# Head norms by narrow matmul tiles, key copies ahead of weight casts, and attention one fill later, in a two-block model step

## The chip, the cores and the metric

The kernel runs on one core of a Trainium2 chip. The metric is the device time of one execution in microseconds. Engines are called as in the profile: PE (TensorE, the matmuls; PEld is its weight load), DVE (VectorE), ACT (ScalarE), POOL (GpSimd), SP (SyncE, which here issues the transfers). Each engine runs its own instruction list in the written order, and the lists are tied together by semaphores alone.

## What is computed

A sequence of 256 tokens of width 1024 goes through two blocks. The change touches the second block only, where a wide projection feeds three branches that are then gated and added:

```
def hgrn2_branch(zq, zi, zf_fwd, zf_bwd, zg, lb, gnorm, w_o):
    ...
    o = one_direction(zf_fwd, lb[0], False) + one_direction(zf_bwd, lb[1], True)
    o = rmsnorm_2(o.transpose(0, 2, 1, 3), gnorm)     # per head: o * rsqrt(mean(o*o) + 1e-6) * gnorm
    gate = jax.nn.silu(zg.astype(f32)).reshape(o.shape)
    o = (o * gate).reshape(b, t, HG_WIDTH).astype(dt)
    return o @ w_o

merged = sigmoid(g_hg) * y_hg + sigmoid(g_na) * y_na + sigmoid(g_ca) * y_ca
```

There are 8 heads of 128 channels in the first branch (HGRN2, "hg"), whose one_direction is a gated scan over the tokens with a decay of its own for each channel, 8 heads of 64 in a neighbourhood attention ("na") and 4 heads of 128 in an attention over 256 memory vectors ("ca").

## The kernel before

**Weights.** All weights come in one order from device memory, as blocks of 128 x 128, 8 to a unit. SP loads two units at a time into `raw` (line 539). ACT rounds a unit into `w_hi` (line 667), then DVE (line 1075) or POOL (line 630) makes the rest, `w_lo`. PE takes the blocks in order and multiplies three times for each: high by high, high by low, low by high (lines 1625 and 1656). `w_hi` and `w_lo` hold four units, so ACT can round a unit only when PE is through with the one four places before; `feed(target)` in ACT's, DVE's and POOL's lists does all units up to a target. Which engine makes `w_lo` is set by a table: DVE for everything in the stretch up to fill ("cq", 1), POOL for the fills mhg 0 and 1 and for all mca and mna fills, both in turn for the rest.

**Fills.** A fill is one bank of PSUM written by PE (16 blocks, 48 three-pass products, or 12 blocks and 36 in the mca and mna fills) and read by ACT or DVE. `wait_fill` in ACT's list first feeds the units whose places the first half of the fill frees, waits for the fill, and feeds the unit that its second half frees. The fills concerned come in the order hi 0-3, hg 0-3, nq 0-1, nk 0-1, nv 0-1, cq 0-1 (the side fills, numbered e = 0 to 15), then mhg 0-7, mca 0-7, mna 0-7 (the merge fills, i = 0 to 23).

**Levels.** The scan of the first branch is done in 7 levels of doubling width, each after a side fill (`LEVEL_AFTER`: levels 0 to 6 after e = 1, 3, 5, 7, 9, 11, 12). For levels 0 to 4 ACT copies keys from `k_fb` into `gate_tmp` and `k_mix` (`level_keys`, line 723) once DVE's `grow` of the level before is done, and PE multiplies from them (line 1883). In ACT's `wait_fill` these copies stand behind the cast of the fill's first half.

**Head norms.** After e = 13, PE's `hg_values` makes the outputs of two heads at a time (g = 0 to 3, lines 1905 and 1906) in PSUM bank `sc[g]`; ACT squares them (929) and copies them out (930); PE multiplies the squares by a 128 x 128 matrix of 1/128 (1912), which puts the mean into all 128 partitions; ACT takes the root (933), DVE the reciprocal (1434), and DVE multiplies the gated outputs by it (1438, gating in 1428). ACT rounds the product into `o_hg_s` (`hg_hi_part`, 938) and DVE makes its low half (1089). The merge fill mhg 0 needs all of `o_hg_s` in its second half.

**Attention.** The 12 heads (4 ca, then 8 na) go through a pipeline in slots: in slot i PE makes the scores of head i (1950; for na two heads at a time, 1939), transposes head i-1's probabilities (1960) and multiplies head i-2's by the values (1985, 1975). DVE finds the maxima (1463, 1465) and normalizes (1470, 1472), ACT takes the exponentials (969). Slot 0 stands before mhg 0 and slot i+1 after merge fill i.

## Time and profile before

| | us |
|---|---|
| median of 3 runs | 934.26 |
| lowest and highest | 931.34, 935.6 |
| the profiled execution's own time | 935.25 |
| its span, first to last instruction | 933.4 |
| PE busy in it | 903.3 |
| DVE, ACT, POOL busy in it | 671.3, 507.1, 305.0 |

The trace's clock starts at the first instruction, so that its end, 933.4, lies 1.85 us under the profiled execution's own time. A matmul's end is modelled, and successive matmuls overlap: the pitch from one start to the next is the price, not the duration. In float32 one product of the program is two MATMUL rows in the trace.

### The profile page before, as it was taken

What the parts mean: (1) busy time and instruction counts of PE and PEld (TensorE: products, weight loads), DVE (VectorE), ACT (ScalarE), POOL (GpSimd) and SP (SyncE); (2) the same over time, 40 slices, a digit from 0 to 9 for tenths busy, and PEclk for the clock granted to TensorE, in tenths of its full rate; (3) what the DMA queues carried; (4) which work ended last, traced back from release to release, by engine and by line L of the source; (5) the groups of instructions that cost most, each with busy time, mean ns of one, the idle gap of its engine ahead of it and who ended that gap; (6) DMA issues with size and microseconds to landing.
All of it is one profiled execution on the core that took longest, in us unless ns stands there. A gap on an engine that the chain in (4) does not pass through costs nothing.

```text
span 933.4 us, 16400 instructions
## 1 busy us (share of the span) xinstructions
PE 903.3 (97%) x6848; PEld 816.5 (87%) x6848; DVE 671.3 (72%) x836; ACT 507.1 (54%) x748; POOL 305.0 (33%) x115
## 2 busy tenths in 40 slices
PE   7998999999999999999999999999999999999996
PEld 7988986888888878999999998998999888888885
DVE  4999677888883257668778778876555589999622
ACT  6544637544554356655554675555545466666542
POOL 2000000565565410000000004845785156666542
PEclk9999999999999999999999999999999999999998
DMA  9583453655555545545535444344455365555551
GB/s 358 208 259 119 147 207 123 236 181 183 191 201 193 190 171 180 180 153 177 197 110 182 161 96 175 137 136 136 136 204 181 137 207 190 192 194 186 185 176 45
DMA packets 31801, 163.78 MB, mean 175 GB/s; under 512 B 9169, under 2 KB 10977, under 8 KB 13296
## 3 DMA queue, kind: packets, MB, share of 16 engines
q1 hardware_dynamic: 31664, 162.66, 50.8%
q8 instruction: 54, 0.88, 0.4%
q14 instruction: 19, 0.16, 0.0%
q0 software_dynamic: 64, 0.08, 0.0%
HBM read 161.32 MB, written 1.42 MB: 174 GB/s over the span
## 4 chain that ended last, share of the span: by engine, by line
PE 80%; DVE 12%; ACT 3%; DMA 2%; issue 1%; SPq 1%; DVEq 0%; ACTq 0%
PE ring L1625 27%; PE acc L1703 18%; PE acc L1637 9%; PE ring L1637 9%; PE acc L1638 4%; PE ring L1638 4%; DVE w_lo L1075 3%; PE ring L1656 3%; DVE conv_y L1167 3%; DMA raw<-wstream 2%; PE acc L1883 1%; ACT w_hi L667 1%; DVE y L1127 1%; DVE ret_inv L1241 1%; ACT sq L673 1%
## 5 line engine op out<-in xcount | busy, mean ns | idle before, releaser
L630 POOL TENSOR_TENSOR w_lo<-raw,w_hi 128x1024 fp32r<-128x1024 f32 x100 | 287.7, 2880 | 595.3 <-ACT w_hi L667 595.1
L667 ACT CAST w_hi<-raw 128x1024 fp32r<-128x1024 f32 x284 | 297.2, 1051 | 312.5 <-PE ring L1625 127.8
L1075 DVE TENSOR_TENSOR w_lo<-raw,w_hi 128x1024 fp32r<-128x1024 f32 x184 | 227.7, 1251 | 112.6 <-ACT w_hi L667 102.3
L1625 PE MATMUL ring<-h,w_hi 128*128 128x256 f32 x1408 | 259.2, 286 | 3.5 <-DVE w_lo L1075 1.8
L1625 PEld LDWEIGHTS ring<-h,w_hi 128*128 128x128 f32 x1408 | 220.8, 192 | 7.3 <-issue 6.4
L1625 PE MATMUL ring<-h,w_lo 128*128 128x256 f32 x704 | 199.9, 284 | 1.1 <-issue 1.1
L1625 PEld LDWEIGHTS ring<-h,w_lo 128*128 128x128 f32 x704 | 135.5, 192 | 0.0
L1637 PE MATMUL acc<-h,w_hi 128*128 128x512 f32 x352 | 124.7, 397 | 0.8 <-DVE h L1133 0.8
L1637 PE MATMUL ring<-h,w_hi 128*128 128x512 f32 x352 | 124.2, 396 | 0.0
L1638 PE MATMUL acc<-h,w_lo 128*128 128x256 f32 x352 | 98.2, 279 | 0.0
L1638 PE MATMUL ring<-h,w_lo 128*128 128x256 f32 x352 | 98.2, 279 | 0.0
L1703 PE MATMUL acc<-w_hi,ff 128*128 128x512 f32 x352 | 94.3, 390 | 0.0
L1637 PEld LDWEIGHTS acc<-h,w_hi 128*128 128x128 f32 x352 | 66.1, 188 | 17.1 <-DVE h L1133 1.0
L1637 PEld LDWEIGHTS ring<-h,w_hi 128*128 128x128 f32 x352 | 66.1, 188 | 15.9
L1703 PEld LDWEIGHTS acc<-w_hi,ff 128*128 128x128 f32 x352 | 65.8, 188 | 13.8 <-DVE w_lo L1075 0.3
L1289 DVE TENSOR_TENSOR ff<-prod_tmp,ff 128x256 fp32r<-128x256 f32 x44 | 67.2, 1530 | 0.9 <-ACT ff L1038 0.9
L1638 PEld LDWEIGHTS acc<-h,w_lo 128*128 128x128 f32 x352 | 66.2, 188 | 0.2 <-issue 0.2
L1638 PEld LDWEIGHTS ring<-h,w_lo 128*128 128x128 f32 x352 | 66.2, 188 | 0.0
L1703 PE MATMUL acc<-w_lo,ff 128*128 128x512 f32 x176 | 54.2, 389 | 0.0
L1656 PE MATMUL ring<-w_hi,h 128*128 128x256 f32 x256 | 48.3, 291 | 0.8 <-ACT v_ret L740 0.8
L1656 PEld LDWEIGHTS ring<-w_hi,h 128*128 128x128 f32 x256 | 41.0, 197 | 1.7 <-ACT v_ret L740 1.0
L1703 PEld LDWEIGHTS acc<-w_lo,ff 128*128 128x128 f32 x176 | 33.0, 188 | 7.0
(252 smaller groups left out, 1269.9 us busy)
## 6 DMA issues: line engine op xcount, KB each, us to landing
raw<-wstream SPq DMA_DIRECT2D x142, 1024.0 KB, 4.9
toep_t<-toep SPq DMA_DIRECT2D x16, 96.0 KB, 3.2
u<-uconv SPq DMA_DIRECT2D x4, 284.0 KB, 6.5
x<-x_tok SPq DMA_DIRECT2D x2, 512.0 KB, 5.1
mem<-mem_tok SPq DMA_DIRECT2D x1, 1024.0 KB, 11.8
w_ple<-wproj SPq DMA_DIRECT2D x1, 1024.0 KB, 6.9
out_t<-y SPq DMA_DIRECT2D x4, 256.0 KB, 2.2
decay<-decay_tab SPq DMA_DIRECT2D x1, 768.0 KB, 6.4
```

The source lines that it names most:

```text
L630: nc.gpsimd.tensor_tensor(w_lo[:, u % UNITS], unit_of_raw(u), as_f32(w_hi[:, u % UNITS]), ALU.subtract).then_inc(lo_ready["pool"], 1)
L667: nc.scalar.copy(w_hi[:, u % UNITS], unit_of_raw(u)).then_inc(hi_ready, 1)
L673: A(spare_out, src, ACT.Square, scale=1.0 / 32.0, accum_out=sums[:, 0, n:n + 1]).then_inc(mean_ready, 1)
L1075: V.tensor_tensor(w_lo[:, u % UNITS], unit_of_raw(u), as_f32(w_hi[:, u % UNITS]), ALU.subtract).then_inc(lo_ready["dve"], 1)
L1127: V.scalar_tensor_tensor(out=y_tok[:, tt, c], in0=src[:, tt, c], scalar=r, in1=gain[name][:, c], op0=ALU.mult, op1=ALU.mult).then_inc(sign ...
L1167: ins = V.scalar_tensor_tensor(out=conv_y[:, j], in0=src, scalar=weight, in1=conv_y[:, j], op0=ALU.mult, op1=ALU.add)
L1289: V.tensor_tensor(ff[:, 1, j], prod_tmp[:, j % 2], as_f32(ff[:, 0, j]), ALU.subtract).then_inc(ff_ready, 1)
L1625: last = mm(dst, w[a], src[:, b, kt], start=n == 0 and i == 0, stop=n == kts - 1 and i == 2)
L1637: mm(both, w[0], h_both[:, kt].rearrange("p a s -> p (a s)"), start=kt == 0, stop=False)
L1638: last = mm(b[:, i, 0], w[1], h[:, 0, kt], start=False, stop=kt == KT - 1)
L1656: last = mm(b[:, tt], src[:, xa, kt, tt * P:tt * P + P], ws[kt][wa], start=kt == 0 and i == 0, stop=kt == KT - 1 and i == 2)
L1703: last = mm(acc[:, tt, 512 * g:512 * g + 512], src(b, i, tt), w[:, u % UNITS, 4 * g:4 * g + 4].rearrange("p a b -> p (a b)"), start=i == 0 ...
```

## The change

It makes five edits.

1. In ACT's `wait_fill` the key copies of a level come before the cast of the fill's first half.
2. The head means of four heads go into one group of matmuls that use only 32 columns of the matrix each and write to 32 partitions each of bank `st` (`hg_mean`), once for heads 0 to 3 behind the third pair of outputs and once for heads 4 to 7 behind the fourth.
3. ACT's root and DVE's reciprocal work on that compact form: two of 128 x 256 each instead of four of 128 x 512. `hg_spread_roots`, behind fill cq 0, multiplies each head's 32 rows of it by 32 rows of 1/128, so that a quarter of the root lands in all 128 partitions of `sc`; DVE multiplies by it and by 4 (`spread_root` names the place).
4. The rounding of `o_hg_s` in ACT and its low half in DVE move behind fill cq 0, all four pairs in a row.
5. Attention slot i stands after merge fill i. `att_scores` of the first two heads waits for all of `hg_out`.

```diff
--- before.py
+++ after.py
@@ -494,6 +495,11 @@
         NHEADS = len(HEADS)
         MERGE_FILLS = [(name, j) for name, j, _, _ in FILLS if name in ("mhg", "mna", "mca")]
 
+        def spread_root(g):
+
+            banks = acc[:, g % 2].rearrange("p (b c) -> p b c", b=2)
+            return banks[:, :, g // 2 * S:g // 2 * S + S]
+
         def unit_of_raw(u):
             return raw[:, (u // 2) % RAW, UB * (u % 2):UB * (u % 2) + UB]
 
@@ -725,10 +731,10 @@
             def wait_fill(name, j, behind=True):
 
                 n = fi(name, j)
-                feed(split_target(n))
                 side = n - fi("hi", 0)
                 if LEVEL_AFTER.get(side, MASKED) < MASKED:
                     level_keys(LEVEL_AFTER[side])
+                feed(split_target(n))
                 act.wait_ge(pe_step, fill_step(n))
                 if behind:
                     feed(behind_target(n))
@@ -922,16 +928,15 @@
                                    sc[g][:].rearrange("p (a b) -> p a b", a=2)).then_inc(st_cross, 1)
 
             def hg_outputs():
-                for g in range(5):
-                    if g < 4:
-                        act.wait_ge(sc_done, SC_HGO + g + 1)
-                        o = sc[g][:].rearrange("p (a b) -> p a b", a=2)
-                        A(hg_sq[:, 2 * g:2 * g + 2], o, ACT.Square).then_inc(hg_squares, 1)
-                        nc.scalar.copy(o_hg[:, 2 * g:2 * g + 2], o).then_inc(o_copied, 1)
-                    if g:
-                        act.wait_ge(hg_stat, g)
-                        A(hg_sq[:, 2 * g - 2:2 * g], sc[g - 1][:].rearrange("p (a b) -> p a b", a=2), ACT.Sqrt,
-                          bias=eps[:, 0:1]).then_inc(hg_root, 1)
+                for g in range(4):
+                    act.wait_ge(sc_done, SC_HGO + g + 1)
+                    o = sc[g][:].rearrange("p (a b) -> p a b", a=2)
+                    A(hg_sq[:, 2 * g:2 * g + 2], o, ACT.Square).then_inc(hg_squares, 1)
+                    nc.scalar.copy(o_hg[:, 2 * g:2 * g + 2], o).then_inc(o_copied, 1)
+                    if g >= 2:
+                        half = slice((g - 2) * S, (g - 1) * S)
+                        act.wait_ge(hg_stat, g - 1)
+                        A(rstd[:, half], st[:, half], ACT.Sqrt, bias=eps[:, 0:1]).then_inc(hg_root, 1)
 
             def hg_hi_part(g):
                 act.wait_ge(hg_out, g + 1)
@@ -954,9 +959,9 @@
                 if e == CROSS_AFTER:
                     cross()
                     hg_outputs()
-                if e >= CROSS_AFTER:
-                    hg_hi_part(e - CROSS_AFTER)
-            hg_hi_part(3)
+                if e == CROSS_AFTER + 1:
+                    for g in range(4):
+                        hg_hi_part(g)
 
             def att_exp(a):
 
@@ -999,7 +1004,6 @@
                 act.wait_ge(merge_full, j + 1)
                 nc.scalar.copy(merged_s[:, 0, j], merged[:, j]).then_inc(merge_hi, 1)
 
-            att_slot(0)
             for i, (name, j) in enumerate(MERGE_FILLS):
                 wait_fill(name, j)
                 wait_gate_slot(act, name, j)
@@ -1007,7 +1011,7 @@
                 A(gate_tmp[:, gate_slot(name, j), 0], bank(name, j)[:, 0], ACT.Tanh, scale=0.5).then_inc(gate_done, 1)
                 if i >= 17:
                     merge_split(i - 17)
-                att_slot(i + 1)
+                att_slot(i)
             merge_split(7)
             prime(ACT.Sqrt)
             feed(end_unit("wout2"))
@@ -1421,24 +1425,27 @@
                     grow(LEVEL_AFTER[e])
                 if e == CROSS_AFTER:
                     gated = []
-                    for g in range(6):
+                    for g in range(4):
+                        dve.wait_ge(o_copied, RET + g + 1)
+                        o = o_hg[:, 2 * g:2 * g + 2]
+                        gated.append(link(V.scalar_tensor_tensor(out=o, in0=o, scalar=col("gnorm"),
+                                                                 in1=gate_hg[:, 2 * g:2 * g + 2],
+                                                                 op0=ALU.mult, op1=ALU.mult)))
+                        if g >= 2:
+                            half = rstd[:, (g - 2) * S:(g - 1) * S]
+                            dve.wait_ge(hg_root, g - 1)
+                            V.reciprocal(half, half).then_inc(hg_inv, 1)
+                if e == CROSS_AFTER + 1:
+                    for g in range(5):
                         if g < 4:
-                            dve.wait_ge(o_copied, RET + g + 1)
+                            dve.wait_ge(hg_spread, 1)
+                            after(gated[g])
                             o = o_hg[:, 2 * g:2 * g + 2]
-                            gated.append(link(V.scalar_tensor_tensor(out=o, in0=o, scalar=col("gnorm"),
-                                                                     in1=gate_hg[:, 2 * g:2 * g + 2],
-                                                                     op0=ALU.mult, op1=ALU.mult)))
-                        if 1 <= g < 5:
-                            dve.wait_ge(hg_root, g)
-                            root_g = hg_sq[:, 2 * g - 2:2 * g]
-                            V.reciprocal(root_g, root_g).then_inc(hg_inv, 1)
-                            dve.wait_ge(hg_inv, g)
-                            after(gated[g - 1])
-                            o = o_hg[:, 2 * g - 2:2 * g]
-                            V.tensor_tensor(o, o, root_g, ALU.mult).then_inc(hg_out, 1)
-                        if g >= 2:
-                            dve.wait_ge(hg_hi, g - 1)
-                            lo_part(o_hg_s, o_hg[:, 2 * g - 4:2 * g - 2], 2 * g - 4, 2 * g - 2).then_inc(hg_split, 1)
+                            V.scalar_tensor_tensor(out=o, in0=spread_root(g), scalar=4.0, in1=o, op0=ALU.mult,
+                                                   op1=ALU.mult).then_inc(hg_out, 1)
+                        if g:
+                            dve.wait_ge(hg_hi, g)
+                            lo_part(o_hg_s, o_hg[:, 2 * g - 2:2 * g], 2 * g - 2, 2 * g).then_inc(hg_split, 1)
 
 
             def att_logits(a):
@@ -1483,9 +1490,6 @@
                 dve.wait_ge(o_att, n + 1)
                 V.tensor_tensor(o[:, 1, t], sc[3][:, 0:S], as_f32(o[:, 0, t]), ALU.subtract).then_inc(att_ready, 1)
 
-            att_logits(0)
-            att_norm(0)
-
             def merge_lo(j):
                 dve.wait_ge(merge_hi, j + 1)
                 V.tensor_tensor(merged_s[:, 1, j], merged[:, j], as_f32(merged_s[:, 0, j]), ALU.subtract
@@ -1494,8 +1498,8 @@
             added = {}
             for i, (name, j) in enumerate(MERGE_FILLS):
                 gates[0] += 1
-                if i + 1 < NHEADS:
-                    att_logits(i + 1)
+                if i < NHEADS:
+                    att_logits(i)
                 feed_behind(name, j)
                 wait_gate(gates[0])
                 yv = bank(name, j)[:, 1]
@@ -1519,10 +1523,10 @@
                         ins.then_inc(merge_full, 1)
                     else:
                         added[i] = link(ins)
-                if i + 1 < NHEADS:
-                    att_norm(i + 1)
-                if 2 <= i + 1 < NHEADS + 2:
-                    att_lo(i - 1)
+                if i < NHEADS:
+                    att_norm(i)
+                if 2 <= i < NHEADS + 2:
+                    att_lo(i - 2)
                 if i >= 17:
                     merge_lo(i - 17)
             merge_lo(7)
@@ -1895,24 +1899,44 @@
                                   start=True, stop=True)
                     last.then_inc(sc_done, 1)
 
+            def hg_value(g):
+
+                pe.wait_ge(st_cross, g + 1)
+                for a in range(2):
+                    hd = 2 * g + a
+                    o = sc[g][:, a * S:a * S + S]
+                    mm(o, v_hg[:, 0, hd * P:hd * P + P], st_hg[:, hd, 0:S], start=True, stop=False)
+                    last = mm(o, v_hg[:, 1, hd * P:hd * P + P], st_hg[:, hd, S:2 * S], start=False, stop=True)
+                last.then_inc(sc_done, 1)
+
+            def hg_mean(half):
+
+                pe.wait_ge(hg_squares, 2 * half + 2)
+                if half:
+                    pe.wait_ge(hg_root, 1)
+                for n in range(4):
+                    last = mm(st[32 * n:32 * n + 32, half * S:half * S + S], mat("m128")[:, 0:32],
+                              hg_sq[:, 4 * half + n], start=True, stop=True)
+                last.then_inc(hg_stat, 1)
+
             def hg_values():
-                for g in range(5):
-                    if g < 4:
-                        pe.wait_ge(st_cross, g + 1)
-                        for a in range(2):
-                            hd = 2 * g + a
-                            o = sc[g][:, a * S:a * S + S]
-                            mm(o, v_hg[:, 0, hd * P:hd * P + P], st_hg[:, hd, 0:S], start=True, stop=False)
-                            last = mm(o, v_hg[:, 1, hd * P:hd * P + P], st_hg[:, hd, S:2 * S], start=False, stop=True)
-                        last.then_inc(sc_done, 1)
-                    if g:
-                        pe.wait_ge(hg_squares, g)
-                        pe.wait_ge(o_copied, RET + g)
-                        for a in range(2):
-                            last = mm(sc[g - 1][:, a * S:a * S + S], mat("m128"), hg_sq[:, 2 * (g - 1) + a],
-                                      start=True, stop=True)
-                        last.then_inc(hg_stat, 1)
-
+
+                for g in range(3):
+                    hg_value(g)
+                hg_mean(0)
+                hg_value(3)
+                hg_mean(1)
+
+            def hg_spread_roots():
+
+                pe.wait_ge(o_copied, RET + 4)
+                for half in range(2):
+                    pe.wait_ge(hg_inv, half + 1)
+                    for n in range(4):
+                        rows = slice(32 * n, 32 * n + 32)
+                        last = mm(sc[n][:, half * S:half * S + S],
+                                  mat("m128")[rows], rstd[rows, half * S:half * S + S], start=True, stop=True)
+                last.then_inc(hg_spread, 1)
 
             for e, (name, j) in enumerate(SIDE_FILLS):
                 if name in ("hi", "nv"):
@@ -1927,6 +1951,8 @@
                     cross()
                     wait_read(pe, "hi", 3)
                     hg_values()
+                if e == CROSS_AFTER + 1:
+                    hg_spread_roots()
 
             def att_scores(a):
                 kind, i = HEADS[a]
@@ -1942,7 +1968,7 @@
                                 last.then_inc(scored, 1)
                     return
                 if a < 2:
-                    pe.wait_ge(hg_root, 4)
+                    pe.wait_ge(hg_out, 4)
                     wait_read(pe, "cq", 1)
                 else:
                     pe.wait_ge(exp_ready, a - 1)
@@ -1994,7 +2020,6 @@
                 if 2 <= i < NHEADS + 2:
                     att_values(i - 2)
 
-            att_slot(0)
             for i, (name, j) in enumerate(MERGE_FILLS):
                 b = open_fill(name, j)
                 tile_out(b[:, 0], h)
@@ -2006,7 +2031,7 @@
                 else:
                     pe.wait_ge(att_ready, 8)
                     tile_out(b[:, 1], o_na, 4)
-                att_slot(i + 1)
+                att_slot(i)
 
             def merged_kt(i, tt):
                 if tt == 0:
```

ACT's list around the side fill e = 3 and the level behind it; `v_hg` is the fill's copy, `gate_tmp` and `k_mix` the key copies, `w_hi` the weight casts. Before:

```order
L740 COPY v_hg<-ring 128x2x256
L667 CAST w_hi<-raw 128x1024
L723 COPY gate_tmp<-k_fb 128x1024
L723 COPY k_mix<-k_fb 128x1024
L667 CAST w_hi<-raw 128x1024
```

After:

```order
L746 COPY v_hg<-ring 128x2x256
L729 COPY gate_tmp<-k_fb 128x1024
L729 COPY k_mix<-k_fb 128x1024
L673 CAST w_hi<-raw 128x1024 x2
L746 COPY v_hg<-ring 128x2x256
```

The two key copies stand ahead of the cast that they stood behind.

PE's list where the head outputs (`acc<-st_hg,v_hg`) and means (`hg_sq,con`) are made, from the third pair of heads on. Before:

```order
L1912 MATMUL acc<-hg_sq,con 128x256 x2
L1905 MATMUL acc<-st_hg,v_hg 128x256
L1906 MATMUL acc<-st_hg,v_hg 128x256
L1905 MATMUL acc<-st_hg,v_hg 128x256
L1906 MATMUL acc<-st_hg,v_hg 128x256
L1912 MATMUL acc<-hg_sq,con 128x256 x4
L1625 MATMUL ring<-h,w_hi 128x256 x2
```

After, with the spread of the roots behind fill cq 0:

```order
L1918 MATMUL ring<-hg_sq,con 32x256 x4
L1908 MATMUL acc<-st_hg,v_hg 128x256
L1909 MATMUL acc<-st_hg,v_hg 128x256
L1908 MATMUL acc<-st_hg,v_hg 128x256
L1909 MATMUL acc<-st_hg,v_hg 128x256
L1918 MATMUL ring<-hg_sq,con 32x256 x4
...
L1629 MATMUL ring<-h,w_lo 128x256
L1937 MATMUL acc<-rstd,con 128x256 x8
L1629 MATMUL ring<-h,w_hi 128x256 x2
```

Eight products over 128 columns became eight over 32, in two groups, and eight products from 32 rows were added between fills cq 0 and cq 1.

ACT's list from the last root to the first merge fill; `q_ca` is the copy of a cq fill, `o_hg_s` the rounding of a pair of heads. Before:

```order
L933 ACTIVATE hg_sq<-acc,eps 128x512 x2
L938 CAST o_hg_s<-o_hg 128x512
L667 CAST w_hi<-raw 128x1024 x2
L740 COPY q_ca<-ring 128x512
L938 CAST o_hg_s<-o_hg 128x512
L667 CAST w_hi<-raw 128x1024 x2
L740 COPY q_ca<-ring 128x512
L938 CAST o_hg_s<-o_hg 128x512 x2
L969 ACT_TABLE_LOAD
```

After:

```order
L939 ACTIVATE rstd<-ring,eps 128x256
L673 CAST w_hi<-raw 128x1024 x2
L746 COPY q_ca<-ring 128x512
L943 CAST o_hg_s<-o_hg 128x512 x4
L673 CAST w_hi<-raw 128x1024 x2
L746 COPY q_ca<-ring 128x512
L673 CAST w_hi<-raw 128x1024 x2
L1011 ACT_TABLE_LOAD
```

All four roundings stand between the copies of cq 0 and cq 1, ahead of the two weight casts of the fill mhg 1, and attention's exponential is no longer ahead of the first merge fill's casts.

## Rows read from the trace of the kernel before

**Rows 1.** The page's part 1: busy us (share), instructions.

```profile
PE 903.3 (97%) x6848; PEld 816.5 (87%) x6848; DVE 671.3 (72%) x836; ACT 507.1 (54%) x748; POOL 305.0 (33%) x115
```

**Rows 2.** PE's waits, 440 to 720 us: who waited for whom, us, times, longest.

```profile
PE acc L1883 <- issue: 1.8, 1, 1.8
PE acc L1950 <- ACT q_ca L740: 1.8, 1, 1.8
PE ring L1625 <- issue: 1.1, 1, 1.1
PE acc L1883 <- ACT gate_tmp L723: 1.0, 1, 1.0
PE acc L1960 <- DVE probs L1472: 0.5, 1, 0.5
PE acc L1912 <- ACT o_hg L930: 0.4, 1, 0.4
...
PE acc L1883 <- ACT k_mix L723: 0.2, 1, 0.2
```

**Rows 3.** Stretches behind e = 1: us; busy PE, PEld, DVE, ACT, POOL; clock, DMA, GB/s.

```profile
460.90:462.70 1.80, 0.02 (x2) 0.00 (x0) 0.34 (x1) 1.80 (x3) 0.00 (x0) 1.00 0.00 0
...
464.20:467.40 3.20, 3.20 (x17) 3.20 (x17) 3.20 (x4) 0.00 (x0) 0.00 (x0) 0.50 0.83 294
```

**Rows 4.** Timeline at e = 3, ACT (start, us, engine, line, operation, [idle before]).

```profile
475.56 1.05 ACT L667 CAST w_hi<-raw 128x1024 fp32r<-128x1024 f32 x1 [2.79 <-PE ring L1656]
476.52 1.23 ACT L723 COPY gate_tmp<-k_fb 128x1024 f32<-128x1024 f32 x1
477.64 1.18 ACT L723 COPY k_mix<-k_fb 128x1024 f32<-128x1024 f32 x1
```

**Rows 5.** Chain of work through the head norms: start, us, what.

```profile
550.61 0.67 PE acc L1905 x2
...
559.51 0.60 ACT hg_sq L929
560.11 0.49 ACT o_hg L930
...
560.73 1.10 PE acc L1912 x4
561.83 11.52 PE ring L1625 x96
```

**Rows 6.** An earlier group of 32-column products: ns min/median/max, first and last start.

```profile
L1737 PE MATMUL acc<-u,w_conv x128: 377/379/405, 64.9 to 71.6; 128*32 128x256 f32 x128
```

**Rows 7.** The chain at attention's scores: ca and na.

```profile
581.96 0.87 PE acc L1950 x4
...
604.84 1.06 PE acc L1939 x8
```

**Rows 8.** Timeline at the end of fill cq 1, ACT and PE.

```profile
573.43 1.04 ACT L667 CAST w_hi<-raw 128x1024 fp32r<-128x1024 f32 x1 [1.83 <-PE ring L1625]
574.38 0.58 ACT L740 COPY q_ca<-ring 128x512 f32<-128x512 f32 x1
...
575.10 1.10 PE L1950 MATMUL acc<-mem_k,q_ca 128*128 128x256 f32 x4 [1.77 <-ACT q_ca L740]
```

**Rows 9.** DVE and POOL in the head norms.

```profile
556.11 3.35 DVE L1434 RECIPROCAL hg_sq<-hg_sq 128x512 f32<-128x512 f32 x1
569.40 2.37 DVE L1438 TENSOR_TENSOR o_hg<-o_hg,hg_sq 128x512 f32<-128x512 f32 x1
...
568.79 2.42 POOL L630 TENSOR_TENSOR w_lo<-raw,w_hi 128x1024 fp32r<-128x1024 f32 x1 [0.43 <-ACT w_hi L667]
```

**Rows 10.** DVE and POOL at head 10, behind merge fill i = 9.

```profile
647.96 0.76 DVE L1455 SCALAR_TENSOR_TENSOR probs<-acc,toep_t 128x256 f32<-128x256 f32 x2 [2.01 <-PE acc L1939]
649.47 1.81 DVE L1465 TENSOR_SCALAR soft<-soft 128x2 f32<-128x2 f32 x1
652.64 0.62 DVE L1472 TENSOR_SCALAR probs<-probs,soft 128x256 f32<-128x256 f32 x2
...
646.51 4.74 POOL L630 TENSOR_TENSOR w_lo<-raw,w_hi 128x1024 fp32r<-128x1024 f32 x2 [2.92 <-ACT w_hi L667]
```

1 line of the change is left out of this document (added).

## The prediction

> **What bounds the kernel now.** The page's first part comes first: PE is busy 903.3 of 933.4 us, the next engine 671.3 [rows 1]. So PE's own list is the bound, the time is its work plus its gaps, and an edit is worth what it takes out of one or the other; time saved on DVE or ACT counts only where PE waits for it. The second view is PE's waits over the stretch that the change touches, 440 to 720 us [rows 2]. They are eight, 7.1 us together, of which the rows show seven: 1.8 and 1.1 us for "issue" (nothing that the profile shows), 1.8 for the copy of `q_ca`, 1.0 and 0.2 for key copies, 0.5 for normalized probabilities, 0.4 for the last copy of a head output. Third, the stretches around the largest gap [rows 3]: PE does nothing from 460.9 to 462.7, and from 464.2 to 467.4 the granted clock is 0.50, that is 1.2 GHz instead of 2.4. Fourth, the chain and the timelines at the places that the diff moves [rows 4, 5, 8, 10].
>
> **Key copies first.** At e = 3 ACT casts a unit at 475.56 for 1.05 us, having idled 2.79 us for PE to free its place, and only then copies keys, until 478.82 [rows 4]. PE waits 1.0 and 0.2 us for them [rows 2]. In the new order the copies can run in ACT's 2.79 idle microseconds: they take 1.23 + 1.18 = 2.4, so they end before the cast can start, and the cast is not later than now. Both waits go: **-1.2 us**. At e = 5, 7 and 9 PE shows no wait for keys, so there is nothing to win; there the casts stand up to 2 us later, and what hides that is the four-unit lead (the unit belongs to the fill after next, over 5 us away). If this cover failed, PE would wait out the rest, at most 2 us at each of three places. At e = 1 the 1.8 us gap falls inside the level's products too, but its row names no copy, so I leave it and the low clock behind it as they are (rival one).
>
> **Means in narrow tiles.** Before, the mean of one head is two MATMUL rows of 128 x 256 at full price. The price is the pitch, which the chain shows as 0.87 us for 4 rows, 0.217 each [rows 7]. Eight heads are 16 rows, 3.45 us. In the new form each product uses 32 columns. The trace has such a group, the packed convolution: 128 rows of 32 columns by 256 start between 64.9 and 71.6, 6.7 / 127 = 0.053 us each, four times as dense [rows 6]. Two groups of 8 rows are then 2 x 0.43; I add 0.15 to 0.2 to each for going into and out of it: the na scores, 8 rows in 1.06 us [rows 7], are 0.19 over 8 x 0.108. That makes 2 x 0.6 = 1.2 us, 2.2 less than now. The wait for ACT changes too. Before, PE waits for the square (0.60) and the copy (0.49) of the last pair, partly filled by another pair's mean, 0.4 us net [rows 2, 5]. Now it needs only the square, but nothing stands in between: 0.60 and some 0.15 to get there and back, 0.75 us. ACT's first compact root is done by then, since it follows the third pair's copy. Sum: -2.2 + 0.35, **-1.9 us**. Bounds: if the groups ran at the full 0.217, they would take 3.45 again and the edit would cost 0.35; at the best, without the 0.2s, it gives 2.3.
>
> **The spread.** New work on PE, between cq 0 and cq 1: eight products from 32 rows, 16 MATMUL rows. No row of the trace has 32-row tiles with 128 columns. Nearest are the na scores, 64 rows and 128 columns, two tiles at once: 8 in 1.06 us, 0.133 each [rows 7]; and the 32-column group at 0.053 [rows 6]. Four different row groups and four banks are used here, so I take 16 x 0.053 + 0.2 = **+1.1 us**. At the two-tile pitch it is 2.1, at the full pitch 16 x 0.217 = 3.5, and nothing excludes that; the low end is 0.85. It waits for DVE's reciprocals, and these have time: a reciprocal of 128 x 512 takes 3.35 us [rows 9], two of half the size the same together, and fill cq 0 gives some 5.8 us (the two cq fills take 11.52, [rows 5]). The 10 us that DVE saves (13.4 of reciprocals become 3.4) are on no path of PE.
>
> The Trainium skill, page "TensorEngine Tiling (Array Packing)", Key Properties, speaks against edits 2 and 3: changing the tiling mode drains the engine. There are six changes here. The measured na group bounds what two of them cost, 0.19 us, and that is in the sum; a price per drain is on no such row, and at a whole matmul's duration of 0.38 each, as in [rows 6], the six would be 2.3 us instead of 0.6.
>
> **Casts behind, and q_ca.** Before, attention's slot 0 follows fill cq 1 at once. PE waits 1.77 us, because ACT casts a unit first (until 574.47) and copies `q_ca` then [rows 8]. In the new order fill mhg 0 starts there, and needs only weights that were cast long before: **-1.8 us**. What is late next? mhg 0's second half, 2.9 us in, needs `o_hg_s`. By the sums above cq 0 ends at about 565.4, the spread at 566.5. DVE then has four products and four low halves of 0.6 to 0.75 us, 5.4 us, and one hold-up: the row at 569.40 took 2.37 us and ended when POOL's cast of 568.79 to 571.21 was through [rows 9], where such a row alone takes 0.69. So the last low half is ready by about 574, and the first pair by 570. PE enters mhg 0 at some 572.3 and its second half at 575.2, taking the pairs one after another: covered by 1 us for the last and 5 for the first. In ACT the four roundings hold the queue until about 572; behind them stand the two casts of mhg 1, with POOL's low parts (2.4 us each) behind these: done by 578.1, needed from 579 and 582. If the cover is gone, PE waits for POOL, one low part of 2.4 us at most. SP's loads wait for these low parts in turn; they are for units four fills on.
>
> The Trainium skill, "SBUF — State Buffer", Who interferes with whom, says that a DVE operation with both inputs in SBUF and a GpSimd operation lock each other out for a whole instruction. The trace agrees (2.37 against 0.69). By this rule the new product, with one input in PSUM, is free of it and only the low halves can be held up.
>
> **Attention a fill later.** No work is added. The wait of 0.5 us at head 10 [rows 2] has this build: its scores come behind fill i = 9, the next fill is a short one, and DVE's scaling of the maxima (1.81 us for 128 x 2 values) sat behind POOL's double cast 646.51 to 651.25 [rows 10]. In the new order the even na heads 8 and 10 follow fills 8 and 10, where POOL has one cast and then a pause, so this hold-up passes to the odd heads, which have one slot more. Worked through, heads 8, 9 and 11 come out with about 0.4 us to spare. I take **-0.2 us**, between -0.5 and +1.
>
> **Sum.** -1.2 - 1.9 + 1.1 - 1.8 - 0.2 = -4.0 us on the profiled span of 933.4, or 935.25 with what lies around it. The median of the runs is 934.26, 1 us under the profiled execution. The saving is the same: 930.3.
>
> **Rivals.**
> 1. *The gap at e = 1 goes too.* For it: the copies for level 0 stand at that place, and the order there changes. PE would win the 1.8 us gap and what the 1.2 GHz cost (half of 3.4 us, 1.7). 930.3 - 3.5 = 926.8. Against it: PE's list is the same up to there, the gap lies in mid-group, and the row says "issue".
> 2. *The narrow tiles do not overlap.* The spread costs 2.1 to 3.5 instead of 1.1: 931.3 to 932.7, "no change". For it: no row shows this shape.
> 3. *The q_ca wait comes back at mhg 0,* as a wait for `o_hg_s` or for mhg 1's weights: the 1.8 us are given back, 932.1. This is the case in which the edit doesn't do what it says. For it: four pairs in a row on one path PE-DVE-ACT-DVE with 1 us of cover. Against: DVE has little else there.
> 4. *Attention becomes late, and the change is slower.* One more na pair works beside the short fills, where POOL is busy more than half of the time. If each of heads 8 to 11 meets a POOL cast in its scaling and another in its normalization, that is 2 x 2.4 less the 0.4 of cover, 4.4 us a head, 17.6 in all, 947.9 at worst. Slower by over 0.5% (938.9) begins at 8.6 us of new waits, so it decides when half of these hold-ups happen: 939 and more. Against it: before, three of the four heads had no wait at all.
>
> **How the numbers follow.** Chances: the forecast 0.50, rival one 0.15, two 0.15, three 0.15, four 0.05. A measurement of this kernel can tell about 0.5% from no change, 4.7 us here; the line is at 929.6. The forecast lies 0.7 above the line, and with 1.5 us of doubt in its terms and in two medians it falls below it in somewhat under half of its cases (0.5 x 0.45 = 0.23). With rival one that is 0.38 for faster. Rivals two and three and the rest of the forecast are 0.57, rival four 0.05 for slower. The range goes from rival one (926.6) to the dear end of rival two (933.0). The forecast's own range is 928.8 to 931.8.
>
> **What would show it.** In the changed profile: no PE wait for `gate_tmp` or `k_mix` behind e = 3; two groups of 8 MATMUL rows on `hg_sq` with starts 0.05 us apart, one wait of 0.75 us for the last square; the 16 rows on `rstd` within 1.1 us; no wait for `q_ca`, nor for `o_hg_s`, between fill cq 1 and the end of mhg 1; the 1.8 us "issue" gap and the 0.50 clock still behind e = 1; PE's waits for normalized probabilities under 0.5 us in all. The forecast is wrong if the gap at e = 1 is gone, if the rows on `rstd` start over 0.1 us apart, or if PE's waits grow between 640 and 665 us.

## The result and the profile after

| | before | after |
|---|---|---|
| median of 6 runs, us | 934.6 | 928.38 |
| lowest and highest | 931.34, 935.6 | 926.34, 929.86 |
| the profiled execution's own time | 935.25 | 929.86 |
| its span | 933.4 | 928.0 |

The ratio is 0.9934, with a 95% interval from 0.9916 to 0.9952, so 4.5 to 7.9 us less. The second set of six runs of the same changed kernel (`after_again`, below) gives 0.9947 [0.9929, 0.9964]. The change is faster by about 0.6%; the forecast was 4.0 us, 0.43%.

The page of the kernel after, part 1, answers to [rows 1]; PE has 16 MATMUL rows more, the spread:

```profile
PE 901.5 (97%) x6864; PEld 813.9 (88%) x6864; DVE 663.8 (72%) x834; ACT 506.1 (55%) x746; POOL 304.7 (33%) x115
```

PE's waits of the kernel after, 440 to 720 us (who waited for whom, us, times, longest), answer to [rows 2]. L1887 is a level, L1629 the fill, L1918 a mean, L1908 a head output:

```profile
PE acc L1887 <- issue: 1.9, 1, 1.9
PE ring L1629 <- issue: 0.8, 1, 0.8
PE ring L1918 <- ACT hg_sq L934: 0.7, 1, 0.7
PE acc L1908 <- ACT st_hg L927: 0.3, 1, 0.3
```

Four waits are left of eight. Both key waits, the one for `q_ca` and the one for the probabilities are gone, the one for a head's copy has become one for its square, as foreseen. No wait stands for `o_hg_s`, mhg 1's weights or the roots. What remains is mostly "issue".

ACT at e = 3, timeline of the kernel after, answers to [rows 4]:

```profile
474.81 0.58 ACT L746 COPY v_hg<-ring 128x512 f32<-128x512 f32 x1
475.29 1.26 ACT L729 COPY gate_tmp<-k_fb 128x1024 f32<-128x1024 f32 x1
476.43 1.18 ACT L729 COPY k_mix<-k_fb 128x1024 f32<-128x1024 f32 x1
478.18 1.05 ACT L673 CAST w_hi<-raw 128x1024 fp32r<-128x1024 f32 x1 [0.57 <-PE ring L1660]
```

The copies take 2.3 us of the time in which ACT had idled 2.79; 0.57 us of idle time is left ahead of the cast, which is still released by PE. So the cast isn't later for them.

The head norms in the chain of work of the kernel after (start, us, what), answering to [rows 5], and the spread's rows (ns min/median/max, first to last start):

```profile
551.49 0.67 PE acc L1908 x2
...
556.91 0.57 PE ring L1918 x8
...
559.44 0.61 ACT hg_sq L934
560.04 0.04 issue
560.09 0.64 PE ring L1918 x8
560.73 5.94 PE ring L1629 x48
566.67 1.08 PE acc L1937 x16
```

```profile
L1937 PE MATMUL acc<-rstd,con x16: 374/374/478, 566.6 to 567.4; 32*128 32x256 f32 x16
```

From the first head output to fill cq 0 it is 560.73 - 551.49 = 9.24 us in the chain now, and cq 0 began at 561.83 - 550.61 = 11.22 in [rows 5]. Of these 1.98 us, 0.28 are the modelled end of the last mean, which the chain counts: from the start of the first output's row to the start of the first row of cq 0 it is 10.87 before and 9.17 now, 1.70 less. In the chain the two groups of eight take 0.57 and 0.64 us, and the sixteen rows of the spread 1.08. By the starts of the same rows of cq 0 and cq 1 (11.57 us before, 12.75 now) the spread costs 1.18.

DVE and ACT behind fill cq 0 and POOL beside them, timelines of the kernel after; [rows 8, 9] are the places before:

```profile
567.81 1.29 DVE L1444 SCALAR_TENSOR_TENSOR o_hg<-acc,o_hg 128x512 f32<-128x512 f32 x2 [4.75 <-PE acc L1937]
569.19 1.65 DVE L1093 TENSOR_TENSOR o_hg_s<-o_hg,o_hg_s 128x512 fp32r<-128x512 f32 x1
570.76 0.68 DVE L1444 SCALAR_TENSOR_TENSOR o_hg<-acc,o_hg 128x512 f32<-128x512 f32 x1
...
572.56 1.46 DVE L1093 TENSOR_TENSOR o_hg_s<-o_hg,o_hg_s 128x512 fp32r<-128x512 f32 x2
```

```profile
573.20 2.00 ACT L673 CAST w_hi<-raw 128x1024 fp32r<-128x1024 f32 x2
```

```profile
567.88 2.41 POOL L636 TENSOR_TENSOR w_lo<-raw,w_hi 128x1024 fp32r<-128x1024 f32 x1 [0.48 <-ACT w_hi L673]
574.33 4.78 POOL L636 TENSOR_TENSOR w_lo<-raw,w_hi 128x1024 fp32r<-128x1024 f32 x2 [4.04 <-ACT w_hi L673]
```

The last low half is done at 574.02. PE began fill mhg 0 at 573.5 and came to its second half 2.9 us later, at 576.4: 2.4 us of cover, where the prediction had 1.

**Where the 5.4 us between the two traces lie.** The table cuts both spans at the starts of the same MATMUL rows. The wide stages are the two long runs of products over 512 columns (line 1637 before, 1641 now), about 155 to 280 and 735 to 860 us; the changed stretch runs from the first product of the diagonal (behind e = 1) to the first product on `merged_s`.

| stretch | before | after | difference |
|---|---|---|---|
| up to the first block's output projection | 122.20 | 122.62 | +0.42 |
| first wide stage | 122.08 | 124.42 | +2.34 |
| diagonal to the first head output | 91.85 | 89.96 | -1.89 |
| from there to the first product on `merged_s` | 162.18 | 159.20 | -2.98 |
| second wide stage | 124.08 | 121.76 | -2.32 |
| last matmul's start to the end | 8.37 | 7.41 | -0.96 |

The rest, some 300 us in four stretches, agrees within 0.1 us in all. The changed stretch gives -4.9 us. Outside of it stand differences that belong to no work of the edits: 1 us at the very end (see "The end of the program" below), 2.3 us up and down again in the wide stages, and 0.4 us up to the first projection, whose start lies between 121.45 and 122.68 us in the fourteen traces of this study, the two of this one program at 122.62 and 121.97.

### The profile page after: what moved, and what is told of

Its sections match the earlier page's. It is cut to its first block, busy times and chain, and to the rows that moved or that the text cites. A ratio compares the mean times of both kernels' runs of the same rounds, so it can differ in the third digit from the quotient of the medians.

```text
span 928.0 us, 16426 instructions
## 1 busy us (share of the span) xinstructions
PE 901.5 (97%) x6864; PEld 813.9 (88%) x6864; DVE 663.8 (72%) x834; ACT 506.1 (55%) x746; POOL 304.7 (33%) x115
## 3 DMA queue, kind: packets, MB, share of 16 engines
HBM read 161.32 MB, written 1.42 MB: 175 GB/s over the span
## 4 chain that ended last, share of the span: by engine, by line
PE 82%; DVE 13%; ACT 3%; issue 1%; DMA 1%; SPq 0%; DVEq 0%; ACTq 0%
PE ring L1629 28%; PE acc L1707 18%; PE acc L1641 9%; PE ring L1641 9%; PE acc L1642 4%; PE ring L1642 4%; DVE w_lo L1079 3%; PE ring L1660 3%; DVE conv_y L1171 3%; PE acc L1887 1%; DVE y L1131 1%; DVE ret_inv L1245 1%; ACT sq L679 1%; DMA gain_mix_pre<-gains 1%; ACT w_hi L673 1%
## 5 line engine op out<-in xcount | busy, mean ns | idle before, releaser
L1629 PE MATMUL ring<-h,w_hi 128*128 128x256 f32 x1408 | 259.2, 286 | 3.6 <-DVE w_lo L1079 1.9
L1629 PEld LDWEIGHTS ring<-h,w_hi 128*128 128x128 f32 x1408 | 220.9, 193 | 7.8 <-issue 7.3
L1629 PE MATMUL ring<-h,w_lo 128*128 128x256 f32 x704 | 199.9, 284 | 0.8 <-issue 0.8
L1629 PEld LDWEIGHTS ring<-h,w_lo 128*128 128x128 f32 x704 | 135.6, 193 | 0.0
```

The lines of the kernel that those rows point to most:

```text
L1629: last = mm(dst, w[a], src[:, b, kt], start=n == 0 and i == 0, stop=n == kts - 1 and i == 2)
```

## The experiments

Each ratio is to the kernel before, in runs interleaved on the same chip. "Tail" is the time from the last matmul's start to the trace's end, "stretch" the two changed stretches of the table above.

| kernel | median us | ratio, 95% interval | both stretches | tail |
|---|---|---|---|---|
| `keys_only` | 931.3 | 0.9981 [0.9965, 0.9997] | 252.26 | 8.39 |
| `att_only` | 931.87 | 0.9991 [0.9979, 1.0004] | 253.00 | 8.35 |
| `norm_only` | 930.54 | 0.9979 [0.9963, 0.9995] | 253.23 | 7.42 |
| `after_again` | 928.01 | 0.9947 [0.9929, 0.9964] | 247.82 | 7.40 |
| `mean_wide` | 929.94 | 0.9969 [0.9954, 0.9983] | 251.94 | 7.41 |
| `spread_twice` | 927.63 | 0.9949 [0.9932, 0.9967] | 248.56 | 7.41 |
| `before_sem` | 933.31 | 1.0005 [0.9992, 1.0017] | 251.99 | 8.36 |
| `act_pad` | 929.95 | 0.9955 [0.9934, 0.9976] | 247.69 | 7.41 |
| `dve_pad` | 929.04 | 0.9954 [0.9939, 0.9969] | 248.43 | 8.35 |
| `before_diag` | 933.46 | 1.0003 [0.9986, 1.002] | | 8.37 |
| `diag_early` | 925.65 | 0.9924 [0.9909, 0.9938] | | 7.40 |
| `level_shift` | 924.36 | 0.9908 [0.9882, 0.9933] | | 7.40 |

(In the last three the diagonal stands elsewhere, so that the stretch isn't the same.)

**The edits one by one.** `keys_only` is the kernel before with edit 1:

```diff
-                feed(split_target(n))
                 side = n - fi("hi", 0)
                 if LEVEL_AFTER.get(side, MASKED) < MASKED:
                     level_keys(LEVEL_AFTER[side])
+                feed(split_target(n))
```

> The kernel before with edit 1 alone (key copies ahead of the cast). My theory: PE's waits for gate_tmp and k_mix behind e = 3 go and nothing else moves; in the trace of after that stretch, from the end of e = 2's level gap to the start of e = 4, was 1.48 us shorter, so -1.5 us on about 934. The issue gap behind e = 1 (1.8 us) and the 0.50 clock after it stay. Rival (the gap at e = 1 belongs to the keys): it goes as well, -5 us in all.

Measured: both waits for keys are gone, all the others stay, and the first of the two stretches is 1.78 us shorter than before. The ratio agrees. The rival is out, since the gap at e = 1 is still there:

```profile
PE acc L1883 <- issue: 2.1, 1, 2.1
```

Row by row, the edit gives 1.7 us: 1.5 at level 1's group and 0.2 ahead of level 0's first product, which starts 0.26 us behind the diagonal's last in the kernel before and 0.06 here. The other 0.1 us is the two "issue" gaps and the stretch at the 0.50 clock, which differ a little in every execution.

`att_only` is the kernel before with edit 5, attention one fill later:

```diff
-            att_slot(0)
             for i, (name, j) in enumerate(MERGE_FILLS):
...
-                att_slot(i + 1)
+                att_slot(i)
```

(and the same in DVE's and PE's lists, lines 1486 to 1525 and 1997 to 2009 of the kernel before).

> The kernel before with edit 5 alone (attention slot i behind merge fill i; the norms as they were). My theory, that the compact norms are the cover for this edit: the waits for q_ca (1.77) and for head 10's probabilities (0.5) go, but mhg 0 now starts near 573.2, its second half reaches the third pair of o_hg_s near 577.5, and that is ready at 578.2 only (the before trace), so a new wait of about 0.7 us stands in mhg 0: -1.6 us. Rival (the edits add up, no cover needed): -2.3 us and no PE wait for o_hg_s.

From the first head output to `merged_s` it took 160.60 us instead of 162.18, -1.58. The waits for `q_ca` and for the probabilities went, and PE's waits of `att_only` show a new one in fill mhg 0's second half:

```profile
PE ring L1621 <- DVE o_hg_s L1088: 0.5, 1, 0.5
```

So rival three was real in this form: with the wide roots and reciprocals in place `o_hg_s` comes 0.5 us late. Edits 2 to 4, worth next to nothing to PE by themselves, are what gives mhg 0 its cover. How much of it is the 10 us that DVE saves, and how much the new places of the roundings, wasn't separated.

`norm_only` is the changed kernel with edits 1 and 5 undone:

```diff
+            att_slot(0)
             for i, (name, j) in enumerate(MERGE_FILLS):
...
-                att_slot(i)
+                att_slot(i + 1)
```

> The changed kernel with edits 1 and 5 undone: narrow means, spread roots and the casts behind cq 0 alone. My theory: the means give -1.7, the spread costs +1.1, and the wait for q_ca before slot 0 grows from 1.8 to about 2.3, because ACT's four roundings and two casts now stand ahead of that copy: together -0.1 us, no change. Rival (these edits carry their own gain): -0.6 to -0.8 us with an unchanged q_ca wait. By the trace the wait for q_ca decides it: 2.3 or 1.8.

PE's waits of `norm_only`, 440 to 720 us:

```profile
PE acc L1980 <- ACT q_ca L746: 2.1, 1, 2.1
...
PE ring L1922 <- ACT hg_sq L934: 0.7, 1, 0.7
```

The `q_ca` wait grew from 1.8 to 2.1 and was followed by 3.4 us at the 0.50 clock; from the first head output to `merged_s` the kernel is 1.3 us slower than before. A stretch of 3.4 us at that clock cost 1.5 us behind e = 1 (below), so taken alone the norm edits give the stretch next to nothing (1.3 - 1.5 = -0.2), as expected: -1.7 for the means, +1.2 for the spread, +0.4 for the longer wait. They are worth something together with edit 5. The ratio is below one all the same, and 0.95 us of that is the shorter tail. How much more of the 2.0 us belongs to the edits, runs of this spread can't tell.

> The changed kernel once more, on the chip of the three parts. My theory: -4.5 us by the traced region (level 0 to the last product of the merge fills), the rest of the first measurement's -6.2 is not the edits' work, so 0.995 of before within 0.2%. The sum of the three parts alone should be smaller, about -3.2. Rival (the edits act outside that region too): 0.9934 again, and a difference between the traces in the stages before e = 0 or behind the merge fills that always has the same sign.

It repeats the changed kernel. No 0.50 clock stands in its stretch, behind a gap of 1.6 us instead of 1.9, and its two stretches are 1.34 us shorter than those of the first trace; its first wide stage is of the quick pace and its second of the slow one. The ratio came as expected, 0.995 within 0.2%. The sum of the parts did not: the three ratios add up to -0.49%, 4.6 us, not the 3.2 us expected, next to -0.53% for the whole. With intervals of 0.13 to 0.18% on each, and a tail of 0.95 us in one of the parts, this shows neither that the edits add up nor that they don't.

**The price of a narrow tile.** `mean_wide`:

```diff
-                    last = mm(st[32 * n:32 * n + 32, half * S:half * S + S], mat("m128")[:, 0:32],
+                    last = mm(st[:, half * S:half * S + S], mat("m128"),
                               hg_sq[:, 4 * half + n], start=True, stop=True)
```

> The changed kernel with the means over all 128 columns of the matrix again, each product written to all 128 partitions of the same place, so that the four heads of a half overwrite each other and the roots are those of one head of four (the compact placement is left out; the number of products, their order and all that follows is kept). Theory (the narrow tile is what makes the means cheap): the rows go from 0.054 to 0.217 us apart, two groups of 8 go from 0.57 and 0.64 to 1.74 each, together +2.2 us. Rival (the gain came from the new grouping and from waiting for the square alone): about 0, groups still near 0.6.

The first group of eight in its chain:

```profile
555.21 1.73 PE ring L1918 x8
```

1.73 against 0.57. From the first head output to `merged_s` 161.32 against 159.20 us, +2.1. The rival is out: the narrow tile is what makes the means cheap, four at a time.

`spread_twice`:

```diff
-                for half in range(2):
+                for half in (0, 1, 0, 1):
```

> The changed kernel with the eight spread products made twice over (32 MATMUL rows instead of 16), to price 32-row tiles of 128 columns. Theory (four row groups work at once): PE's 16 added rows start 0.05 us apart, +0.9 us for the group (1.08 becomes about 1.95), no new wait. Rival (the rows run one after another and the 1.08 us is something else): 16 x 0.217 = +3.5 us. In the time +0.9 is +0.1%, at the edge of what the rounds can tell; the group's pitch in the trace decides.

```profile
L1937 PE MATMUL acc<-rstd,con x32: 374/374/478, 562.4 to 564.0; 32*128 32x256 f32 x32
```

Thirty-two rows start within 1.6 us, and the stretch grew by 0.87 us, 0.054 for each of the sixteen added. Of the 1.18 us that the spread costs, 0.87 is then pitch and 0.3 the way in and out. Tiles of 32 rows by 128 columns overlap four times, like those of 128 rows by 32 columns: in the trace of the kernel after, both kinds start in fours 0.007 us apart, and the next four follow after 0.2 to 0.3 us, about the pitch of a single row at full width (0.216).

**The gap behind e = 1.** The "issue" gap stood behind one MATMUL row, the 3113th (57 rows into level 0), and the second gap behind the 3876th, 20 rows (ten products) after level 3's group, in all eleven traces that have the diagonal behind e = 1, with and without any of the edits. The first was 1.3 to 2.1 us long in them, the second 0.7 to 1.6. The windows of the kernel after (us; busy PE, PEld, DVE, ACT, POOL; clock, DMA, GB/s) answer to [rows 3]:

```profile
463.48:465.34 1.86, 0.00 (x0) 0.00 (x0) 0.53 (x1) 0.24 (x1) 0.00 (x0) 1.00 0.43 57
466.90:470.30 3.40, 3.40 (x18) 3.40 (x17) 3.40 (x4) 0.00 (x0) 0.00 (x0) 0.50 0.37 154
```

ACT was busy all through the gap before (1.80 of 1.80 us) and is busy 0.24 us of it now, and the gap is as long: the key copies aren't its cause. The lower clock behind it cost 1.5 us: the 96 MATMUL rows behind level 0 took 13.0 us here and before, and 11.5 in `after_again` and `act_pad`, where the clock stayed up. When the gap begins, a packet of PE's own instruction list is under way. The page's part 3 of the kernel after counts these packets (number, MB, share), and its DMA view from 462.6 to 466 us has one of them:

```profile
q8 instruction: 54, 0.88, 0.4%
```

```profile
q8 instruction: 1, 0.02, 2.3%
```

54 packets of 16 KB carry PE's list, one for every 128 MATMUL rows with their weight loads (6864 / 54 = 127). No other list is long enough: the trace has 13973 instructions of PE and 2453 of all other engines. And the packets tell when the gaps end. In the eleven traces, the packet that is under way or just through when the gap begins takes 0.9 to 1.4 us, and PE goes on 1.2 to 1.6 us after its end, 22 times out of 22 for the two gaps. The diagonal and level 0 are small products in a row, 128 rows and 128 more, all in 2.5 to 2.9 us of work: two packets' worth, where a fill takes 15 us for one. So the experiment moves the diagonal ahead by one fill, `diag_early` (its expectation counts the weight loads with the products: the diagonal is 128 MATMUL rows, 256 instructions, and so is a level):

```diff
-        DIAGONAL_AFTER, CROSS_AFTER = 1, 13
+        DIAGONAL_AFTER, CROSS_AFTER = 0, 13
```

> The changed kernel with one number altered: the 256 small products of the diagonal (512 MATMUL rows with level 0's) no longer stand directly ahead of level 0's products behind fill e = 1, the diagonal goes behind fill e = 0. Theory A (the 'issue' gap behind e = 1 is PE's instruction supply running dry after a dense run of small products): with a fill between the two runs the gap of 1.3 to 2.1 us and, where it stands, the 0.50 clock behind it go; a wait of at most 0.5 us for the level's data may take the place. About 2 to 3.5 us less than the changed kernel (some 925 us, ratio to the kernel before 0.991). Rival B (the gap belongs to level 0's own copies or to the length of the whole run of side fills, not to the density): the gap stays at the same place in front of level 0 and the time is the changed kernel's, 928.

The chain of `diag_early` at both places:

```profile
452.55 1.30 PE acc L1860 x82
453.85 5.97 PE ring L1660 x48
459.82 1.51 PE acc L1887 x128
461.33 11.71 PE ring L1660 x96
```

All 128 rows of level 0 run in 1.51 us without the gap (the packet that stood beside it is through at 456.85 now, before they start), and the stretch behind them isn't at the lower clock. Theory A holds in the trace: from the diagonal's new place to the first head output it is 93.20 us, against 95.82 in the trace of the kernel after, which had the lower clock, and 94.45 in `after_again`, which didn't. PE's waits have 0.3 us for `q_bf` in exchange. The second gap stays where it was, and is a long one in this execution:

```profile
PE ring L1629 <- issue: 1.6, 1, 1.6
```

The time is 925.65 us, 2.4 to 2.7 under the medians of the changed kernel, but these were taken on other chips; by the ratios (0.9924 against 0.9934 and 0.9947) the gain is 0.9 to 2.1 us, and the intervals overlap. The gain rests on the traces.

The same number altered in the kernel before, `before_diag`:

> The kernel before with one number altered: the diagonal's 256 MATMUL rows go behind fill e = 0 instead of directly ahead of level 0's. Theory A (the 'issue' gap behind e = 1 belongs to PE's dense run of small products): it goes here as it did in the changed kernel, with the 0.50 clock behind it where that stands, the other waits of the kernel before stay (q_ca 1.8, keys 1.0 and 0.2, probabilities 0.5); the sum is 1.3 to 3.4 us, ratio 0.998 to 0.996, and the time stays above the changed kernel's with the same edit (925.65), by 4 to 5 us. Rival B: the gap went only together with the changed order of key copies; here it stays at 1.8 and the ratio is 1.000.

Theory A had the gap right and the time wrong: the gap went here too, but nothing was gained (1.0003). From the diagonal's new place to the first head output it is 95.98 us, against 97.70 in the trace of the kernel before, which had the lower clock, and 95.65 in that of `before_sem`, which didn't. PE's waits of `before_diag`:

```profile
PE acc L1883 <- ACT gate_tmp L723: 2.2, 2, 1.3
...
PE acc L1883 <- ACT k_mix L723: 0.7, 2, 0.4
```

The copies for level 0, which in this kernel stand behind a cast, had been hidden under the diagonal and the gap. Now level 0 waits for them, 1.3 and 0.4 us, next to the waits of level 1 at e = 3, which stood before as well. Putting the diagonal ahead pays only with the key copies first. This is a worth of edit 1 that the prediction didn't see and the changed kernel doesn't use.

`level_shift` has `diag_early`'s edit and moves levels 3 and 4:

```diff
-        LEVEL_AFTER = {1: 0, 3: 1, 5: 2, 7: 3, 9: 4, 11: 5, 12: 6}
-        DIAGONAL_AFTER, CROSS_AFTER = 1, 13
+        LEVEL_AFTER = {1: 0, 3: 1, 5: 2, 8: 3, 10: 4, 11: 5, 12: 6}
+        DIAGONAL_AFTER, CROSS_AFTER = 0, 13
```

> The changed kernel with the diagonal behind e = 0, and levels 3 and 4 one fill later (behind e = 8 and 10 instead of 7 and 9). The second 'issue' gap (0.7 to 1.6 us) stood at the same MATMUL row, the 3876th, in every kernel so far, ten rows behind level 3's group. Theory C (a place in PE's instruction list where the next piece comes late because a dense group ran just ahead): with the group at another place of the list the gap goes or gets another length. Rival D (the gap belongs to level 3's group wherever it stands): it follows ten rows behind the group, behind e = 8. Price of the move: level 4 and level 5 stand one fill apart, so PE may wait up to 2 us for DVE's growth there. Time between 924.5 and 927.5.

PE's waits of `level_shift`, 440 to 720 us:

```profile
PE acc L1887 <- DVE f_fb L1418: 0.9, 1, 0.9
PE ring L1918 <- ACT hg_sq L934: 0.7, 1, 0.7
PE acc L1908 <- ACT st_hg L927: 0.3, 1, 0.3
PE acc L1860 <- DVE q_bf L1384: 0.3, 1, 0.3
```

No "issue" is left, and the gap didn't follow the group: theory C over D, for a wait of 0.9 us between levels 4 and 5. This is one trace; the first gap's absence is shown by three (`before_diag`, `diag_early`, `level_shift`). The traced stretch is 0.96 us shorter than `diag_early`'s. With 924.36 us and 0.9908 it is the fastest kernel of this study; that it beats `diag_early` (0.9924) lies inside the intervals.

**The end of the program.** `before_sem` is the kernel before with one semaphore more:

```diff
+        hg_spread = sem("hg_spread")
```

> The kernel before with one semaphore more that nothing uses. It tests what stands at the program's end: the stretch from the last matmul's start to the trace's end was 8.4 us in the kernel before and in the two variants without the head-norm edits, 7.4 us in the kernels with them. Theory (the extra semaphore, or the program's layout by it, shortens the end): the tail is 7.4 and the time 0.95 us less, ratio 0.999. Rival (the tail goes with the edited work, or has two values of its own): the tail is 8.4, ratio 1.000. The waits in the stretch of the change are those of the kernel before.

The tail stays 8.36: the theory fell. What went with the long tail in all fourteen traces was a packet of the second instruction queue. Its 18 or 19 packets of 8 KB are about as many as the 2453 instructions of all engines but PE need, at the 63 bytes that an instruction of PE's takes (54 x 16384 / 13973), so I take it to carry all those lists (an estimate). The DMA view of the kernel before, its last 3 us, has it; that of the kernel after has none. The page's part 3 counts 19 before and 18 after:

```profile
q14 instruction: 1, 0.01, 1.3%
```

```profile
q14 instruction: 18, 0.15, 0.0%
```

The norm edits take two instructions from ACT and two from DVE, waits counted: the traces list 1052 and then 1050 of ACT, 960 and then 958 of DVE. (The expectations below count 1012, 1010, 962 and 960, with the same differences.) Two kernels give them back, one each. `act_pad`:

```diff
                         A(rstd[:, half], st[:, half], ACT.Sqrt, bias=eps[:, 0:1]).then_inc(hg_root, 1)
+                        act.wait_ge(hg_stat, g - 1)
+                        act.wait_ge(hg_squares, g + 1)
```

> The changed kernel with two spare waits in ACT's list (on semaphores long reached), so that ACT has 1012 instructions again as in the kernel before, not 1010; DVE keeps 960 (962 before). It tests the end of the program: 8.4 us from the last matmul's start to the trace's end in the kernels with ACT 1012 and DVE 962, where an 8 KB instruction piece is loaded inside the span 1.7 us before its end, and 7.4 us in those with 1010 and 960, where that piece comes after the span's end. Theory E (ACT's count crosses the border of a piece): the tail is 8.4 again, +0.95 us, and the page counts 19 packets on the second instruction queue, not 18. Rival F (it is DVE's count, or the work edited): the tail stays 7.4, 18 packets. No other wait changes; in the time 0.1%, less than the rounds tell, so the trace decides.

Tail 7.41, 18 packets: not ACT. `dve_pad`:

```diff
                             V.reciprocal(half, half).then_inc(hg_inv, 1)
+                            dve.wait_ge(hg_root, g - 1)
+                            dve.wait_ge(o_copied, RET + g + 1)
```

> The changed kernel with two spare waits in DVE's list (on semaphores long reached), so that DVE has 962 instructions again as in the kernel before, not 960; ACT keeps 1010. Theory G (the border of an 8 KB instruction piece that DVE's count crosses at the program's end): the tail from the last matmul's start to the trace's end is 8.4 us again instead of 7.4, the last piece of the second instruction queue is loaded about 1.7 us before the trace's end instead of after it, and the page counts 19 packets there, not 18. Rival H (the edited work itself or something else): the tail stays 7.4, 18 packets, and the cause stays open. No other wait changes; +0.95 us is 0.1%, less than the rounds tell, so the trace decides.

Tail 8.35, and the page of `dve_pad` reads:

```profile
q14 instruction: 19, 0.16, 0.0%
```

The last microsecond of the program hangs on two instructions of DVE: a saving of 0.95 us which belongs to no work at all. The traces show where it goes. The program ends when SP has seen the last landing of the output. Up to the output's first transfer all keeps its distance from the last matmul's start (it is issued 4.24 us after it in `before`, `after`, `act_pad` and `dve_pad` alike). In the eight traces with the short tail the last landing is at 7.0 us, and the packet starts at 8.5 us, behind the end. In the six with the long tail the packet starts at 6.6 us, while the output is under way; all landings but one are there by 7.05 us, and the last is at 7.96 to 7.99. That the packet itself holds up this landing is the likely reading; no run isolates it.

## Why the prediction came out as it did

**Key copies first: right, a little small.** Predicted -1.2, measured -1.7. At e = 3 it is 1.5: the gap of 1.0 us ahead of level 1's group is gone, and the group itself took 1.23 us from its first row to the next fill's, not 1.68. The mis-sized term is the second copy's: its late end cost 0.45 us inside the group, where the table of waits shows 0.2. The other 0.2 us were gained at e = 1, ahead of level 0's first product, a wait too short for the table; all traces without edit 1 and with the diagonal in its place have it, and none with edit 1.

**Means in narrow tiles: right.** Predicted -1.9, measured -1.70. With 32 output rows at 0.216 us taken off, the old means and their wait came to 3.96 us by the starts (3.45 + 0.4 in the sum; 16 x 0.217 is 3.47), and the new ones to 2.26 (1.2 + 0.75). The mis-sized term is the new ones': 0.85 us for the wait, and 1.4 for both groups, because the rows beside them start later too (0.31 us apart, not 0.216). The pitch of [rows 6] was the right nearest row, and `mean_wide` shows the other end.

**Spread: right.** Predicted 1.1, measured 1.08 in the chain and 1.18 by the starts around it. Rival two is out. The Trainium skill, "TensorEngine Tiling (Array Packing)", Key Properties, says that changing the tiling mode drains the engine, and gives no price. The way in and out of this group cost 0.3 us, by `spread_twice` against `after`; the sum had 0.2, and two changes at 0.38 each would be 0.76.

**`q_ca`: right.** Predicted -1.8, measured -1.9 by the starts (the wait of 1.77 and the entry into the score's group), with no new wait. The cover was 2.4 us where the prediction had 1, because DVE was through 6.3 us after the spread's rows and not 7.5. (Its clock times at this place leave out the 1.2 us of the keys, which shifts them all alike.) That the wait doesn't come back at mhg 0 is due to the norm edits, as `att_only` shows with its 0.5 us. POOL's cast held one low half, 1.65 us instead of 0.68 to 0.73, and left the two products with an input in PSUM alone (1.29 for two). The Trainium skill, "SBUF — State Buffer", Who interferes with whom, has it so: a DVE instruction with two inputs in SBUF contends with a GpSimd instruction that reads SBUF, one with at most one such input doesn't outside the 2-port modes.

**Attention a fill later: right in kind, too cautious.** Predicted -0.2 between -0.5 and +1, measured -0.5: the wait for probabilities went and none came. The odd heads were held by POOL as expected (DVE's scaling of heads 9 and 11 took 1.62 and 1.63 us, that of heads 8 and 10 0.17), and PE shows no wait for them. Rival four never began.

**The gap at e = 1: rightly left in the sum, rival one wrong for this change.** It stood in the changed kernel, 1.9 us, with the 0.50 clock behind it in one of its two traces. The price of that clock, half of 3.4 us in the prediction, was 1.5.

**Sum.** By the starts of the same rows it is -1.7 (keys) - 1.7 + 1.2 - 1.9 - 0.5 = -4.6, against -4.0. The second "issue" gap was 0.2 us shorter in this execution, which is chance, since it goes from 0.7 to 1.6 from one execution to the next; so the stretch gave 4.87. To this comes the tail's 0.95, of which the prediction knew nothing: it sums PE's waits up to the last product and takes what follows as fixed. -4.6 - 0.95 = -5.6 us, or a ratio of 0.9940, lies between the two measured ones, 0.9934 and 0.9947. So the mechanism was right in each of its terms, the sum was 0.6 us small by them, most of it in the keys and in attention, and 0.95 by one that it lacked.

**Luck.** The forecast's own branch ended at 928.8; the median fell 0.4 us below it, inside of the whole range only because rival one had stretched that to 926.6, and rival one didn't happen. By its terms alone, 4.6 us, the change would be just short of the 0.5% line (4.7 us, 929.6), which the forecast had stood 0.7 above. The tail's 0.95, for which nobody had reasoned, carries it across. The whole range itself ends 0.2 us below (926.6) and 0.3 above (933.0) the sums given for its ends, 926.8 and 932.7.

**The spread of runs.** The two wide stages run at one of two paces, in every kernel. All MATMUL rows of the high parts of the first stage, in the kernel after and in `after_again` (ns min/median/max, first to last start; both traces are of the same program):

```profile
L1641 PE MATMUL ring<-h,w_hi x176: 395/398/403, 161.4 to 279.7; 128*128 128x512 f32 x176
```

```profile
L1641 PE MATMUL ring<-h,w_hi x176: 391/391/391, 160.6 to 276.7; 128*128 128x512 f32 x176
```

118.3 us against 116.1. No wait of more than 0.2 us is shown, the clock is the full one, and the time for the same rows is longer by 2%. Over the fourteen traces the first stage takes 122.1 or 124.4 us and the second 121.8 or 124.1, nothing between, in all four combinations. This is 2.3 us each way, twice; with the 1.5 us of the low clock and the lengths of the two "issue" gaps it is enough for the 4 to 7 us by which the runs of one kernel lie apart. It is why edits of 1 to 2 us are at the edge of what even twelve runs show, and why the traces had to decide. What sets the pace stays open.

## What to carry to other kernels

Sum PE's waits by the rows, and then ask of each gap labelled "issue" which place in the instruction list it stands at. If it is at the same instruction in every trace, and a packet of the list is under way or just through as it begins, spreading dense runs of small products is worth a try (here, for one number, a gap of 1.3 to 2.1 us, and 1.5 more where the low clock followed). Before moving work into a place that it leaves, look at what it had been hiding there: the diagonal hid the key copies, the compact norms hide `o_hg_s`. And an edit's value can lie in what it makes possible: the key order gave 1.7 us, and made room for the diagonal's move, 1.3 to 2.6 more by the traces. Last, ask of a saving which work it belongs to: 0.95 us here belonged to none.
